# Score products over 128 rows with zeros for the other head, and the distance bias added by VectorE

## The reference, cut to what matters

```python
def _dilated_branch(q, k, v, rel_bias, window, dil):
    ...
    bias = rel_bias[_t5_bucket(jnp.maximum(dist, 0) * dil)].transpose(2, 0, 1)
    valid = (dist >= 0) & (dist <= steps) & (key_pos >= 0)
    s = jnp.einsum('nbqhd,nbkhd->nbhqk', qb, kb) / math.sqrt(dh) + bias
    s = jnp.where(valid[None, :, None], s, -jnp.inf)
    m = jnp.max(s, axis=-1)
    p = jnp.exp(s - m[..., None])
```

## Time and profile before

| | before |
|---|---|
| median of three runs | 1687.64 us |
| the profiled execution | 1685.32 us |
| its span | 1683.5 us |
| TensorE matmuls busy | 1628.2 us (97%) |
| VectorE busy | 970.6 us (58%) |
| ScalarE busy | 810.2 us (48%) |
| GpSimd busy | 50.7 us (3%) |
| mean granted TensorE clock | 0.989 |
| the attention stage | about 206 to 356 us of the span |

### The profile page before, as it was taken

The page is one execution under the profiler, slowest core; times in us unless marked ns, Lnnn a source line. Parts: engine busy times, 40 slices in busy tenths (PEclk is TensorE's granted clock), DMA queues, the critical chain, the costliest instruction groups (busy, mean ns, idle before and its releaser), DMA issues.

```text
span 1683.5 us, 19537 instructions
## 1 busy us (share of the span) xinstructions
PE 1628.2 (97%) x7593; PEld 1328.3 (79%) x7593; DVE 970.6 (58%) x1218; ACT 810.2 (48%) x1014; POOL 50.7 (3%) x95
## 2 busy tenths in 40 slices
PE   7999999889999999999999999999999999989999
PEld 6888777678887788878777888787778878777887
DVE  4554566465455555466556554557945565794554
ACT  5543465254444543446655443455354535535552
POOL 2000000000000000000000000001000000100000
PEclk9999999999999999989999999999999999999999
DMA  9644644135547453544435544654424446442443
GB/s 300 219 145 178 222 175 150 50 127 185 174 145 255 164 198 137 189 163 151 149 113 190 176 158 169 202 208 150 150 100 150 150 174 239 150 150 101 148 152 125
DMA packets 187061, 279.29 MB, mean 166 GB/s; under 512 B 8525, under 2 KB 98805, under 8 KB 186992
## 3 DMA queue, kind: packets, MB, share of 16 engines
q1 hardware_dynamic: 184720, 271.27, 46.2%
q0 software_dynamic: 2128, 7.04, 1.4%
q10 hardware_dynamic: 144, 0.03, 0.0%
HBM read 277.26 MB, written 1.06 MB: 165 GB/s over the span
## 4 chain that ended last, share of the span: by engine, by line
PE 79%; DVE 13%; ACT 5%; issue 2%; POOL 1%; DMA 0%; POOLq 0%; SPq 0%; ACTq 0%; DVEq 0%
PE ACC L738 20%; PE ACC L740 20%; PE ACC L739 20%; DVE WL L1891 5%; PE TB L769 2%; PE ZB L914 2%; ACT WH L1304 2%; PE ACC L947 2%; PE ACC L949 1%; PE ACC L948 1%; PE ACC L1047 1%; PE ACC L1049 1%; PE ACC L1048 1%; ACT XH L1335 1%; PE ZB L917 1%
## 5 line engine op out<-in xcount | busy, mean ns | idle before, releaser
L1891 DVE TENSOR_TENSOR WL<-RAW,WH 128x2048 fp32r<-128x2048 f32 (+3 forms) x258 | 508.1, 2012 | 271.8 <-ACT WH L1304 267.5
L738 PE MATMUL ACC<-WL,XH 128*128 128x512 f32 (+2 forms) x1312 | 518.2, 395 | 16.8 <-issue 6.5
L740 PE MATMUL ACC<-WH,XL 128*128 128x512 f32 (+2 forms) x1312 | 509.4, 388 | 0.0
L739 PE MATMUL ACC<-WH,XH 128*128 128x512 f32 (+2 forms) x1312 | 508.7, 388 | 0.0
L1304 ACT ACTIVATE WH<-RAW 128x2048 fp32r<-128x2048 f32 (+3 forms) x258 | 422.4, 1687 | 163.4 <-PE ACC L740 109.3
L738 PEld LDWEIGHTS ACC<-WL,XH 128*128 128x128 f32 x1312 | 249.7, 190 | 75.0 <-issue 14.7
L740 PEld LDWEIGHTS ACC<-WH,XL 128*128 128x128 f32 x1312 | 249.5, 190 | 51.3
L739 PEld LDWEIGHTS ACC<-WH,XH 128*128 128x128 f32 x1312 | 249.9, 190 | 47.1
L738 PE MATMUL ACC<-WL,HH 128*128 128x512 f32 x352 | 138.1, 392 | 0.5
L740 PE MATMUL ACC<-WH,HL 128*128 128x512 f32 x352 | 137.1, 389 | 0.0
L739 PE MATMUL ACC<-WH,HH 128*128 128x512 f32 x352 | 137.1, 389 | 0.0
(11 more groups left out here) (293 smaller groups left out, 1800.2 us busy)
## 6 DMA issues: line engine op xcount, KB each, us to landing
RAW<-w_in_in SPq DMA_DIRECT2D x68, 1024.0 KB, 6.5
RAW<-ffn_w_gate_in SPq DMA_DIRECT2D x43, 1024.0 KB, 5.2
RAW<-ffn_w_up_in SPq DMA_DIRECT2D x43, 1024.0 KB, 7.4
RAW<-ffn_w_down_in SPq DMA_DIRECT2D x32, 512.0 KB, 4.5
RAW<-ffn_w_down_in SPq DMA_DIRECT2D x16, 1024.0 KB, 6.8
RAW<-mlstm_w_in_in SPq DMA_DIRECT2D x16, 1024.0 KB, 7.2
RAW<-ffn_w_down_in SPq DMA_DIRECT2D x16, 768.0 KB, 5.7
RAW<-attn_w_in_in SPq DMA_DIRECT2D x12, 1024.0 KB, 6.1
```

The costliest lines, as they stand in the source:

```text
L738: nc.tensor.matmul(bank, lh, wl[:, i, :], start=first and i == 0, stop=False)
L739: nc.tensor.matmul(bank, lh, wh[:, i, :], start=False, stop=False)
L740: mm = nc.tensor.matmul(bank, ll, wh[:, i, :], start=False, stop=last and i == k - 1)
L1891: nc.vector.tensor_tensor(WL[:, slot, lo:hi], RAW[:, slot, lo:hi], WH[:, slot, lo:hi].bitcast(F32), ALU.subtract).then_inc(lo_ready, 1)
```

## The change

Queries go to a new tile QZ that has a [128 x 256] tile for each head: the head's 64 partitions hold its transposed queries and the other 64 hold zeros. Keys stay two heads to a tile, in KT. `scores` multiplies all 128 partitions; the zeros take the other head out. GpSimd writes the zeros with two memsets of 64 partitions by 2048 elements each, after the row scales and ahead of the store of the bias rows; TensorE waits for them before unit 0. VectorE copies a query group by two instructions of 64 partitions instead of one of 128.

The second product of the dilated units is gone. VectorE adds the bias in `logits`: two additions (128x128 and 128x256) read ZB and BT with the keys in reverse order, and write to UL. The maxima and exponentials read UL. The table is built over distances in the other direction so that the reversed read fits. The wait for BT goes from TensorE to VectorE, and `scores` waits for `logits` of the unit before in every unit. The stage needs 8 KB more per partition; the constants shrink by 128 columns.

```diff
-        QT = sb("QT", [P, 4, 4, SEQ], offset=o)
-        o += 4 * 4 * SEQ * 4
+        QZ = sb("QZ", [P, 2, HEADS, SEQ], offset=o)
+        o += 2 * HEADS * SEQ * 4
+        KT = sb("KT", [P, 2, HEADS // 2, SEQ], offset=o)
+        o += HEADS * SEQ * 4
...
                 def scores(u):
                     side, h = divmod(u, HEADS)
-                    part = slice(DH * (h % 2), DH * (h % 2) + DH)
+                    if u == 0:
+                        pe.wait_ge(queries_zeroed, 2)
                     if h == 0:
                         pe.wait_ge(groups_used, g0 + ATTN_GROUP["staged", 3 * side + 1, 1] + 2)
-                    if u == HEADS:
-                        pe.wait_ge(bias_ready, 16)
                     if u:
-                        pe.wait_ge(logits_ready if u <= HEADS else w_ready, u0 + u)
-                    head_scores(QT[part, 2 * side, h // 2, :], QT[part, 2 * side + 1, h // 2, :], ZB[:, 0:3 * P],
-                                (flip, BT[:, h, :]) if side else None).then_inc(z_ready, 1)
+                        pe.wait_ge(logits_ready, u0 + u)
+                    head_scores(QZ[:, side, h, :], KT[:, side, h // 2, :], ZB[:, 0:3 * P]).then_inc(z_ready, 1)
...
-                        softmax_exp(u, ZB[:, 0:3 * P])
+                        softmax_exp(u, UL[:, u % 2, :])
...
                 rsqrt_of_x()
                 at.rsqrt += 1
+                pool.wait_ge(rsqrts, at.rsqrt)
+                nc.gpsimd.memset(QZ[DH:P, :, 0::2, :], 0.0).then_inc(queries_zeroed, 1)
+                pool.wait_ge(queries_zeroed, 1)
+                nc.gpsimd.memset(QZ[0:DH, :, 1::2, :], 0.0).then_inc(queries_zeroed, 1)
+                pool.wait_ge(queries_zeroed, 2)
                 pool.wait_ge(bias_rows, 1)
...
                 def staged(j):
                     for g in range(2):
-                        at.group = g0 + ATTN_GROUP["staged", j, g]
-                        group_plain(QT[:, {0: 0, 1: 1, 3: 2, 4: 3}[j], 2 * g:2 * g + 2, :].rearrange("p k n -> p (k n)"),
-                                    DH ** -0.5 if j in (0, 3) else None)
+                        t = g0 + ATTN_GROUP["staged", j, g]
+                        dve.wait_ge(groups_ready, t + 1)
+                        src = TB[t % 2][:, :].rearrange("p (k n) -> p k n", k=2)
+                        if j in (0, 3):
+                            for odd in range(2):
+                                rows = slice(DH * odd, DH * odd + DH)
+                                ins = nc.vector.tensor_scalar(QZ[rows, j // 3, 4 * g + odd:4 * g + 4:2, :], src[rows, :, :], DH ** -0.5, None,
+                                                              ALU.mult)
+                        else:
+                            ins = nc.vector.tensor_copy(KT[:, j // 3, 2 * g:2 * g + 2, :], src)
+                        ins.then_inc(groups_used, 1)
 
                 def logits(u):
                     z = ZB[:, 0:3 * P]
                     if u >= HEADS:
                         dve.wait_ge(z_ready, u0 + u + 1)
                         dve.wait_ge(w_ready, u0 + u - 1)
-                        softmax_maxima(u, z)
+                        if u == HEADS:
+                            dve.wait_ge(bias_ready, 16)
+                        l = UL[:, u % 2, :]
+                        for lo, hi in ((0, P), (P, 3 * P)):
+                            ins = nc.vector.tensor_tensor(l[:, lo:hi], z[:, lo:hi], BT[:, u - HEADS, 0:hi - lo][:, ::-1], ALU.add)
+                        step(ins)
+                        softmax_maxima(u, l)
                         return
```

More of the change, by code:

```diff
@@ L109, in shape_constants @@
     far = np.concatenate([free, free, free + P], axis=1)
-    dist = (np.arange(3 * P) - P)[::-1]
+    dist = np.arange(3 * P) - (P - 1)
     onehot = np.zeros((33, 3 * P), np.float32)
@@ L126, in shape_constants @@
     return {"c_onehot": onehot, "c_tiles": np.concatenate([
-        ident, goes_on, past, count, ident[:, ::-1],
+        ident, goes_on, past, count,
         (part <= free).astype(np.float32),
@@ L134 @@
 CONSTANTS = shape_constants()
-C_IDENT, C_GOES_ON, C_PAST, C_COUNT, C_FLIP = 0, P, 4 * P, 7 * P, 10 * P
-C_UPTO, C_AFTER, C_ONE, C_LATER = 11 * P, 12 * P, 13 * P, 13 * P + 1
+C_IDENT, C_GOES_ON, C_PAST, C_COUNT = 0, P, 4 * P, 7 * P
+C_UPTO, C_AFTER, C_ONE, C_LATER = 10 * P, 11 * P, 12 * P, 12 * P + 1
 def program(nc, x, norm_g, ffn_w_gate, ffn_w_up, ffn_w_down, attn_w_in, attn_w_out, rel_bias,
@@ L362, in program @@
         bias_ready = sem("bias_ready")
+        queries_zeroed = sem("queries_zeroed")
         rope_done = sem("rope_done")
@@ L379, in program @@
         count_t = CT[:, C_COUNT:C_COUNT + 3 * P]
-        flip = CT[:, C_FLIP:C_FLIP + P]
         upto = CT[:, C_UPTO:C_UPTO + P]
@@ L915, in head_scores @@
                     if add:
-                        table = add[1][:, lo:hi] if add[1] is MK else add[1][:, SEQ - (hi - lo):]
-                        mm = nc.tensor.matmul(z[:, lo:hi], add[0], table, start=False, stop=True)
+                        mm = nc.tensor.matmul(z[:, lo:hi], add[0], add[1][:, lo:hi], start=False, stop=True)
                 return mm
@@ L2061, in step @@
                 dve.wait_ge(dve_step, steps[0])
[L2063 to L2068, removed]
             def out_product():
```

## The result

The changed kernel takes 0.9938 of the time before (95% interval 0.9924 to 0.9952): a median of 1680.80 us over 18 runs, against 1692.82 us over 18 runs of the kernel before. At 1692.82 us the ratio is a gain of 10.5 us, 8.1 to 12.9. The median lies in the forecast's range (1680.0 to 1687.2) and faster had the greatest chance, but the forecast gain was 4.5 us: the direction was right, the size less than half of it.

A forecast was written before the change was run, and what follows sets the result against it. TensorE, four fifths of the chain, bounds the kernel, except in units 8 to 10, where other engines set the pace. Gains 0.35 + 3.1 + 1.05 = 4.5 us give a 1683.1 us median; range 1680.0 to 1687.2.

The forecast's parts named there:

- The bias products, units 11 to 15: Attention stage: removing 1.05 us of TensorE products a unit saves 0.78 in each of units 11 to 14, 1.05 in 15.
- The wait for the exponentials: Units 11 to 14: a new TensorE wait of 0.27 us before `turn`, as the weights come later than TensorE is ready.
- the shortened scores still hide `masked`: Units 11 to 15: `masked` takes 0.55 us beside scores of 1.04, so `weigh` has no added wait.
- The rows: Scores on TensorE: using 128 partitions instead of 64 at the same columns costs nothing.
- Units 8 to 10: Attention stage, where other engines set the pace: TensorE goes on 0.78 us earlier at half clock, taken as 0.35 us.
- The clock rival: Later stage boundaries: shifted idle gaps make new low-clock time, taking back 1.7 to 3.4 us; 1684.8 to 1686.5 us; chance 0.27.
- The longer chain: VectorE's additions: reversed reads cost as the scan does, 0.35 us more in each of four units; 1684.8 us; chance 0.08.
- the collision: GpSimd's memsets hold up VectorE's weight-tile halves at 214.34, 6.8 us late; 2.3 slower in all, 1689.9 us; chance 0.03.
- the slow memsets: Ahead of unit 0: memsets ending after about 233 delay TensorE and `softplus`; 1703 us at 10 ns an element; chance 0.05.
- The edits costed at nothing: Query copies in two instructions, memsets delaying the bias-row store by 1.5 us, moved BT wait, smaller constants: no cost.

The follow-up runs named there:

- bias_only: The changed kernel with scores multiplying only their head's 64 partitions again, the bias still on VectorE: 1684.80 us, ratio 0.996.
- rows_only: The kernel before with zero-padded queries, so scores multiply 128 partitions, and the bias still a TensorE product: 1679.72 us, ratio 0.994.
- dup64: The kernel before with the scores of units 0 to 7 issued twice in a row, over 64 rows: turns of two units 7.55 us apart.
- dup128: The changed kernel with the scores of units 0 to 7 issued twice in a row, over 128 rows: turns of two units 7.15 us apart.
- fill: The changed kernel with unread 512-column matmuls in TensorE's idle time, two after weigh 8 and two after scores 10: one run, 1682.14 us.
- slow_zeros: The changed kernel with each of GpSimd's two memsets done eight times: attention stage 144.43 us, against 134.75 in the changed kernel.

## Why the prediction was right, and where it was short

- *The bias products, units 11 to 15.* Forecast 0.78 us in each of four units and 1.05 in unit 15. T11 to T15 holds the scores of units 12 to 15, for which that makes 3 x 0.78 + 1.05 = 3.4 us; measured 4.3. For the bias by itself the forecast was close: bias_only saves 3.6 there, with its units 3.59 us apart for 3.69. What comes on top is the rows. Taken in the other order, the rows give 3.1 of the 4.3 and the bias 1.2. The wait for the exponentials is there, of 0.3 us. That the shortened scores still hide `masked` was wrong: `weigh` waits for `masked`, since the scores don't take the 1.04 us that I had given them.
- *The rows.* This is the step that failed: "They now use 128 partitions instead of 64; line 917 does that already at the same columns ... so I cost that at nothing." Line 917's 0.42 and 0.63 us were not the price of 128 rows. They were the price of a product over 128 rows between products over 64, and line 914's was the same from the other side. In rows_only the same line takes 0.22 and 0.43. The row that could have told it was in the trace: the 0.36 and 0.33 us of `issue` on the weight loads around line 914. I took 0.85 us for four matmuls as their length and didn't ask why the next large matmul took 0.43 instead of 0.23. Measured: 3.1 us before T7 for nothing forecast, and in rows_only 3.1 between T11 and T15. The Trainium skill (TensorEngine Tiling (Array Packing), Key Properties) says that a change of the tiling mode drains TensorE. dup64 against dup128 agrees with it: a head pays once, however many products over 64 rows follow each other. That is 0.39 us for two changes, some 0.2 us each (an estimate). It was the rule to weigh here, and I had not weighed it.
- *Units 8 to 10.* Forecast 0.35 us, and 0.78 for unit 11, whose scores lie before T11 too: 1.13; measured 1.6. The shape was right (other engines set the pace, most of the gain is lost), but the scores were shortened by the row change as well, and the time at half clock there grew from 6.8 to 10.2 us. By fill, that low clock cost 2.7 us.
- *Rivals.* The clock rival was misjudged as evidence, not as mechanism: three times within 0.64 us were no proof of little scatter. Eighteen runs of the kernel before spread over 14 us. The scatter is the clock's: 39 more runs of that kernel, made beside the experiments, go from 1684.81 us at a mean granted clock of 0.989 to 1702.23 at 0.979. A clock lower by 0.010 over 1690 us is 17 us, and the two are 17.4 apart. The Trainium skill (TensorE: Matmul & The Clock Gate, Part 1) calls the monitor free-running. That spread agrees with the rule; no run here shows that it is the reason. The longer chain falls (0.62 us for the additions), the collision falls (4.50 us beside the memsets, in slow_zeros too), the slow memsets fall (1.81 us), and slow_zeros shows where they would have counted.
- *The total.* 4.5 forecast; the missing terms are 3.1 before T7, 0.5 from T7 to T11 and 0.9 from T11 to T15, which makes 9.0, the stage's difference. The rest up to 10.5 is within the interval. TensorE was to be busy for 8.4 us less and was for 7.4, at a lower mean clock.
- *The edits costed at nothing* were nothing: four query copies of 0.7 us, the wait for BT, and the store, which starts 13.5 us into the stage before and 13.8 after. It waits for VectorE's copy of the bias rows in both, not for the memsets, which had ended at 217.3.

Open is why the same kernel's clock falls at some boundaries and not at others, and the size of the fillers' gain over the whole kernel.

## What to carry to other kernels

On TensorE, look at the weight load ahead of a short product and behind it: if it starts only after the matmul before, and the product has another row count than its neighbours, padding it with zeros to the neighbours' rows can be worth more than taking a product away. When two edits are made at once, measure each alone: here the lesser-looking one gave all that could be measured in the total, and left the other 1.2 us. And a profile's span is compared at equal clock, stage by stage between fixed marks; three runs close together don't bound the scatter.

## What the runs showed of the hardware

- Four 32-bit matmuls (two of 128 columns, two of 256) with their loads cost 1.05 us between products over 128 rows when they are over 64 rows, and 0.66 when they are over 128; twice as many cost 0.64 to 0.66 more in either case.
- A GpSimd memset of 64 partitions by 2048 32-bit elements took 1.81 us, 0.9 ns an element, and didn't lengthen a VectorE subtraction of two SBUF operands beside it (4.50 us for two).
- VectorE's addition of a PSUM operand and a reversed SBUF operand took what a maximum of the same size did (0.29 and 0.41 us, 0.62 for both).
- Idle matmuls in waits of TensorE held the granted clock at 1.00 where it had been 0.55, and the stretch from turn 7 to turn 11 went from 21.84 us to 19.16 although 3.8 us of work were added. Each was one profiled execution, and another stretch of that same execution lost clock instead.
